# Output projection started on six of eight operand tiles, with the memory's keys and values computed beside its post-norm

## The chip, the cores and the metric

The kernel runs on one core of one Trainium2 chip. It is written by hand, engine by engine, with semaphores. Time is device microseconds of one execution: median 3300.87 us over three runs (3298.69 to 3303.33) for the kernel before. The profiled execution is a run of its own, of 3297.09 us.

## The reference, cut to what matters

A first block (512 tokens, width 1024, one layer) is followed by a second block of two layers. The change touches the middle of each of these two layers:

```python
def second_block(x, mem, ...):
    for l in range(2):
        h = rms_norm(x, mix_pre_g[l]);  proj = h @ w_in[l]
        ...                                            # latent attention (512 wide), gated unit (256 wide)
        o = rms_norm(diff_attention, g_sub) * (1 - lam_init)   # per head of 64; 256 wide
        mix = concat([out_a, out_b, o]) @ w_mix_out[l]         # 1024 x 1024
        x = x + rms_norm(mix, mix_post_g[l])
        h = rms_norm(x, mem_pre_g[l]);  mem_n = rms_norm(mem, mem_kv_g[l])   # mem: 256 tokens
        q = h @ mem_w_q[l];  k, v = split(mem_n @ mem_w_kv[l])
        x = x + rms_norm(attention(q, k, v) @ mem_w_o[l], mem_post_g[l])
        ...                                            # convolutional feed-forward
```

The keys and values need only `mem`, not `x`.

## The kernel before, in words

Activations lie features first: `[128, 8, 512]`, eight tiles `k` of 128 features by 512 tokens. The matrices come as a stream of slabs, 16 blocks of 128x128 each (1 MB). SyncE loads slab after slab into a ring of four (`feed`); ScalarE copies a slab's upper part to fp32r into a ring of two, `ring_hi` (`round`, L223), VectorE subtracts and leaves the lower part in place (`halve`, L230). A product is then three matmuls: upper by upper, upper by lower, lower by upper. Such three matmuls of one block are called a triple here. Activations are split the same way: ScalarE makes `hi`, VectorE (or GpSimd) `lo`. TensorE may begin a slab when `slab_split` has counted it; ScalarE may round the next one when `slab_begun` says that TensorE is past the slab whose place it takes. Each engine works off its instructions in order.

`stage(...)` puts one function on each engine between two barriers. In a layer the stages around the change are:

- `differential`: 16 units `u` of scores S (L1226), four transposes T (L1234), and for two units at once the values product V (L1243). VectorE takes maxima (L1282) and differences (L1292), ScalarE exponentials (L1265) and the copies of the turned tiles (L1271).
- `sub` (`norms`): the norm by heads of its result, `mix` tiles 6 and 7: two squares (L600), two sums on TensorE (L649), twice Ln and Exp, two products on VectorE (L670).
- `mix_out` (`project`, L1509): the eight `mix` tiles are split (L1528, L1541), output tile `n` = 8 triples into PSUM bank `n` (L281); beside it ScalarE squares finished banks (L730) and TensorE sums them (L736, two tiles behind). Then comes `PostNorm`: scale (L544, L546), new `x` on VectorE and GpSimd (L779, L784, L793), its squares (L766), eight sums (L744) and the next scale.
- `mem_qkv` (`linear`): `x` is normed and split, TensorE does four tiles of the query product (L412 to L414), sums the squares of `mem` (L649), does the other four, then eight key tiles of 256 columns and four value products of 512 columns in two groups (all L281).
- `memory`: the attention, which starts with GpSimd's copies (L1016).

The queries' slabs lie in the stream ahead of those of the keys and values, and all are loaded in that order.

## Time and profile before

| what | us |
|---|---|
| median of three runs | 3300.87 |
| profiled execution | 3297.09 |
| its span in the trace | 3295.3 |
| TensorE busy | 3002.6 |
| `differential` to the start of `memory`'s copies, first layer | 1541.41 to 1782.99 |

The span is what the trace shows of the execution; 1.8 us lie around it. Every time given below is counted from the start of the span. The two layers are the same instructions twice, so each figure of the first has its twin about 983 us later.

### The profile page before, as it was taken

How to read it: one execution, taken by the hardware profiler on the slowest of the kernel's cores; microseconds unless marked ns; L12 is line 12 of the kernel's file. 1: busy time of each engine (PE TensorE's matmuls, PEld its weight loads, DVE VectorE, ACT ScalarE, POOL GpSimd, SP SyncE). 2: the span in 40 equal slices, each digit the busy share in tenths (PEclk: the TensorE clock that was granted, in tenths of full speed). 3: DMA queues.
4: the chain of work that ended last, by engine and by line, in shares of the span. 5: the costliest groups of instructions: out<-in, count | busy, mean ns of one | idle time of the engine just before them, and what ended most of it. 6: DMA issues, size and time to landing. Idle time of an engine off the chain costs nothing. (4 is left out here: it accounts for less than half of the span.)

```text
span 3295.3 us, 39545 instructions
## 1 busy us (share of the span) xinstructions
PE 3002.6 (91%) x14872; PEld 2345.1 (71%) x14872; DVE 1519.0 (46%) x2143; ACT 1281.8 (39%) x1848; POOL 348.8 (11%) x299
## 2 busy tenths in 40 slices
PE   6989887999989989999789899988999889899998
PEld 2879765688768876675568678876775568578875
DVE  3356246565444433456444344433466444344432
ACT  3741434522243323435443333323435443433323
POOL 0110004500001100003011011100003011011100
PEclk8999999999999999999899999999999799999999
DMA  5100210044422222210122122221210122122222
GB/s 225 64 26 1 80 55 1 11 163 167 145 77 90 101 78 84 77 64 1 39 77 103 51 90 89 102 86 65 78 64 1 39 77 103 51 90 102 89 98 77
DMA packets 43554, 254.04 MB, mean 77 GB/s; under 512 B 4608, under 2 KB 6784, under 8 KB 15872
## 3 DMA queue, kind: packets, MB, share of 16 engines
q1 hardware_dynamic: 43392, 251.87, 21.5%
q8 instruction: 103, 1.69, 0.2%
q14 instruction: 59, 0.48, 0.1%
HBM read 249.75 MB, written 2.10 MB: 76 GB/s over the span
## 5 line engine op out<-in xcount | busy, mean ns | idle before, releaser
L230 DVE TENSOR_TENSOR ring_lo<-ring,ring_hi 128x2048 fp32r<-128x2048 f32 x201 | 460.6, 2292 | 934.7 <-ACT ring_hi L223 934.7
L281 PE MATMUL bank<-h_hi,ring_hi 128*128 128x512 f32 x1408 | 583.1, 414 | 55.6 <-DVE gated_lo L1488 26.1
L223 ACT ACTIVATE ring_hi<-ring 128x2048 fp32r<-128x2048 f32 x201 | 384.0, 1911 | 544.6 <-PE bank L281 400.7
L281 PE MATMUL bank<-h_hi,ring_lo 128*128 128x512 f32 x1408 | 556.4, 395 | 0.0
L1345 PE MATMUL bank<-h_hi,ring_hi 128*128 128x512 f32 x960 | 374.1, 390 | 5.8 <-DVE ring_lo L230 5.8
L1348 PE MATMUL bank<-h_lo,ring_hi 128*128 128x512 f32 x960 | 373.5, 389 | 0.0
L1349 PE MATMUL bank<-h_hi,ring_lo 128*128 128x512 f32 x960 | 373.5, 389 | 0.0
L281 PEld LDWEIGHTS bank<-h_hi,ring_hi 128*128 128x128 f32 x1408 | 268.6, 191 | 131.2 <-issue 55.7
L281 PEld LDWEIGHTS bank<-h_hi,ring_lo 128*128 128x128 f32 x1408 | 268.5, 191 | 63.4
L281 PE MATMUL bank<-h_lo,ring_hi 128*128 128x512 f32 x560 | 218.9, 391 | 0.0
L1345 PEld LDWEIGHTS bank<-h_hi,ring_hi 128*128 128x128 f32 x960 | 180.2, 188 | 45.8 <-issue 8.3
L281 PE MATMUL bank<-gated_lo,ring_hi 128*128 128x512 f32 x528 | 211.0, 400 | 0.0
L1349 PEld LDWEIGHTS bank<-h_hi,ring_lo 128*128 128x128 f32 x960 | 180.2, 188 | 37.3
L1348 PEld LDWEIGHTS bank<-h_lo,ring_hi 128*128 128x128 f32 x960 | 180.2, 188 | 37.3
L1416 DVE SCALAR_TENSOR_TENSOR mix<-bank,par,mix 128x511 f32<-128x511 f32 x176 | 123.8, 745 | 133.3 <-ACT mix L1393 126.3
L281 PE MATMUL bank<-mix_lo,ring_hi 128*128 128x512 f32 x336 | 143.1, 426 | 6.0 <-PEq L324 6.0
L281 PEld LDWEIGHTS bank<-h_lo,ring_hi 128*128 128x128 f32 x560 | 105.7, 189 | 25.1 <-issue 3.9
L1393 ACT ACTIVATE mix<-bank,par 128x512 f32<-128x512 f32 x88 | 63.7, 774 | 151.3 <-PE bank L1349 151.3
L281 PEld LDWEIGHTS bank<-gated_lo,ring_hi 128*128 128x128 f32 x528 | 100.9, 191 | 24.7 <-issue 2.4
L1430 POOL TENSOR_TENSOR gated<-mix 128x512 f32 (+1 forms) x44 | 57.0, 1296 | 427.5 <-ACT mix L1398 427.5
L1195 POOL TENSOR_TENSOR squares<-squares,stat 128x512 f32<-128x512 f32 x64 | 65.2, 1039 | 331.4 <-DVE stat L1157 331.4
L793 POOL TENSOR_TENSOR xT<-xT,raw 128x512 f32<-128x512 f32 x18 | 27.4, 1524 | 683.1 <-DVE raw L779 683.1
(415 smaller groups left out, 5105.4 us busy)
## 6 DMA issues: line engine op xcount, KB each, us to landing
ring<-in_stream SPq DMA_DIRECT2D x209, 1024.0 KB, 4.8
mod_w<-in_stream SPq DMA_DIRECT2D x64, 256.0 KB, 4.9
xT<-in_xT SPq DMA_DIRECT2D x2, 2048.0 KB, 14.9
const<-in_const SPq DMA_DIRECT2D x1, 2306.5 KB, 16.0
par<-in_par SPq DMA_DIRECT2D x3, 696.0 KB, 3.9
memT<-in_memT SPq DMA_DIRECT2D x2, 1024.0 KB, 4.7
out<-xT SPq DMA_DIRECT2D x1, 2048.0 KB, 6.3
ctxT<-in_ctxT SPq DMA_DIRECT2D x1, 1024.0 KB, 4.9
```

Of the source, the lines that this page charges most:

```text
L223: nc.scalar.activation(self.slab_hi(slab + j), self.slab(slab + j), ACT.Copy).then_inc(slab_rounded, 1)
L230: nc.vector.tensor_tensor(lower, self.slab(slab + j), self.slab_hi(slab + j).bitcast(F32), ALU.subtract)\
L281: ins = nc.tensor.matmul(out, lhsT, rhs, start=start and w is w_hi and x is x_hi, stop=stop and w is w_lo)
L793: nc.gpsimd.tensor_tensor(xT[:, n, :], xT[:, n, :], self.raw[:, n, :], ALU.add)\
L1195: nc.gpsimd.tensor_tensor(p, p, stat[:, u % 2, 2, g:g + 1].to_broadcast([P, p.shape[1]]), ALU.mult)\
L1345: first = nc.tensor.matmul(out_ap[s], w_hi, x_hi, start=k == 0, stop=False)
L1348: nc.tensor.matmul(out_ap[s], w_hi, x_lo, start=False, stop=False)
L1349: last = nc.tensor.matmul(out_ap[s], w_lo, x_hi, start=False, stop=k == KT - 1)
L1393: last = nc.scalar.activation(work[:, j % 2, s, :], out_ap[s], ACT.Identity, bias=conv_b(col), scale=conv_w(2 * FT + col))
L1416: last = nc.vector.scalar_tensor_tensor(w, out_ap[s][:, 1 - lo:T - lo], conv_w(col), w, ALU.mult, ALU.add)
L1430: nc.gpsimd.tensor_tensor(gated(n), work[:, j % 2, 0, :], work[:, j % 2, 1, :], ALU.mult)\
```

## The change

Three things are done in each layer. First, in `differential`, V of units `u-2` and `u-1` is issued ahead of T of unit `u`, not behind it. Second, the stage `sub` is gone, and `project` for `mix_out` is replaced by `mix_and_memory`: output tiles 0 and 1, then 2 and 3, first take their products with operand tiles 0 to 5, and the last two operand tiles follow when they are normed. Third, this same stage also norms and splits `mem`, and while the post-norm of `x` runs, TensorE does the keys and values; `mem_q` with only the queries is a stage of its own after it. GpSimd has no part in this post-norm, the slabs are loaded keys and values first, and some semaphores are shared.

```diff
+AT_MQ = B2_AT["mq"] + KV_SLABS * SLAB
+MQ_FIRST = B2_AT["mq"] // SLAB
+B2_AT["mk"], B2_AT["mv"] = B2_AT["mq"], B2_AT["mq"] + KT * KT
+assert B2_AT["mk"] % SLAB == 0
...
+                        place = g + APART
+                        if 0 <= s - MQ_FIRST < KV_SLABS:
+                            place += MQ_SLABS
+                        elif 0 <= s - MQ_FIRST - KV_SLABS < MQ_SLABS:
+                            place -= KV_SLABS
+                        src = stream[bass.ds(layer[0] * B2_SLABS + place, 1)].rearrange("o p n -> p (o n)")
...
+                if not by_pool:
+                    self.pool_tiles = ()
...
                 for u in range(N + 1):
                     if u + 2 < N:
                         scores(u + 2)
+                    if u >= 2 and u % 2 == 0:
+                        values(u - 2)
                     if u < N:
                         transposes(u)
-                    if u >= 2 and u % 2 == 0:
-                        values(u - 2)
...
+        def mix_and_memory(x, post, memT, mem_hi, mem_lo, k_out, v_out, h_gain, sub_gain, sync):
...
+            TILES, REST = 4, KT - 2
+            at, at_k, at_v = B2_AT["mix"], B2_AT["mk"], B2_AT["mv"]
+            first_k, first_v, first_q = at_k // SLAB, at_v // SLAB, (at_v + KT * KT) // SLAB
+            AHEAD = (4, 5, 6, 7, 0, 1, 2, 3)
...
+            k_banks = (1, 2, 3, 4, 5, 6, 7, 1)
+            v_banks = (2, 3, 4, 5)
...
+            def tensor(pe):
+                def key_tile(j):
+                    if j < len(LEFT):
+                        pe.wait_ge(y_left.sem, y_left.at(j + 1))
+                    elif j < KT - 1:
+                        pe.wait_ge(post.normed.sem, post.normed.at(j - len(LEFT) + 1))
+                    else:
+                        pe.wait_ge(k_read.sem, k_read.at(1))
+                    for k in range(KT):
+                        if j == 0:
+                            pe.wait_ge(mem_split.sem, mem_split.at(k + 1))
+                        last = ws.mm(pe, at_k + j * KT + k, 1, bank[:, k_banks[j], 0:MEM], (mem_hi[:, k, :], mem_lo[:, k, :]),
+                                     True, k == 0, k == KT - 1)
+                    last.then_inc(k_done.sem, 1)
...
+                def value_tiles(half):
+                    pe.wait_ge(k_read.sem, k_read.at(3 if half == 0 else 5))
+                    for k in range(KT):
+                        for tb in range(2):
+                            c = slice(tb * P, (tb + 1) * P)
+                            last = ws.mm(pe, at_v + half * 4 * KT + k * 4, 4, bank[:, v_banks[2 * half + tb], :],
+                                         (mem_hi[:, k, c], mem_lo[:, k, c]), False, k == 0, k == KT - 1)
+                    last.then_inc(v_done.sem, 1)
...
+                def first_tiles():
...
+                    for half in range(2):
+                        pe.wait_ge(slab_split, ws.count(first + half) - WHOLE_SLABS)
+                        for k in range(REST):
+                            for n in (2 * half, 2 * half + 1):
+                                begun = part_of(n, k)
+                                if k == 0 and n == 0:
+                                    begun.then_inc(slab_begun, 1)
+                            if half == 0 and k == 1:
+                                for g in range(2):
+                                    pe.wait_ge(sub_squared.sem, sub_squared.at(g + 1))
+                                    nc.tensor.matmul(bank[:, 6 + g, :], con("ones64"), post.squares[:, 2 + g, :], start=True, stop=True)\
...
+                    for n in range(TILES):
+                        for k in range(REST, KT):
+                            begun = part_of(n, k)
...
+                        if n >= 2:
+                            post.sum(pe, n - 2)
...
+                first_tiles()
+                for n in range(TILES, KT):
+                    if n == TILES:
+                        for k in range(KT):
+                            pe.wait_ge(mem_squared.sem, mem_squared.at(k + 1))
+                            last = nc.tensor.matmul(bank[:, 7, 0:MEM], con("ones"), mem_squares[:, k, :], start=k == 0, stop=k == KT - 1)
...
+                    for k in range(KT):
+                        last = ws.mm(pe, at + n * KT + k, 1, bank[:, n, :], x.part(pe, k), True, k == 0, k == KT - 1)
+                    last.then_inc(post.sum_done.sem, 1)
+                    if n >= 2:
+                        post.sum(pe, n - 2)
+                post.sum(pe, KT - 2)
+                post.sum(pe, KT - 1)
+                for j in range(5):
+                    key_tile(j)
+                next_sums(range(4))
+                for j in range(5, KT):
+                    key_tile(j)
+                next_sums(range(4, KT))
+                value_tiles(0)
+                value_tiles(1)
...
+                ws.round_to(act, at // SLAB, ws.limit)
+                upper(0)
+                upper(1)
+                for g in range(2):
+                    nc.scalar.activation(post.squares[:, 2 + g, :], x.whole[:, REST + g, :], ACT.Square).then_inc(sub_squared.sem, 1)
+                upper(2)
+                upper(3)
+                ws.round_second(act, at // SLAB + 1)
+                upper(4)
+                upper(5)
...
+                for g in range(2):
+                    act.wait_ge(sub_summed.sem, sub_summed.at(g + 1))
+                    nc.scalar.activation(sub_scale[g], bank[:, 6 + g, :], ACT.Ln, bias=con("eps", 1), scale=1.0 / 64)
+                act.drain()
+                for g in range(2):
+                    nc.scalar.activation(sub_scale[g], sub_scale[g], ACT.Exp, scale=-0.5).then_inc(sub_scaled.sem, 1)
+                upper(6)
+                upper(7)
+                act.wait_ge(sync.loaded.sem, sync.loaded.at(16))
...
+                for n in range(KT):
+                    ws.round_to(act, (at + n * KT + KT - 1) // SLAB + 1, ws.limit)
+                    post.square(act, n)
+                    if n in LEFT:
+                        leave(n)
...
+                ws.round_second(act, first_k + 1)
+                post.rms(act)
+                key_out(0)
+                key_out(1)
+                ws.round_to(act, first_k + 2, ws.limit)
+                next_squares((0, 1))
+                key_out(2)
+                key_out(3)
+                ws.round_to(act, first_k + 3, ws.limit)
+                next_squares((2, 3))
+                key_out(4)
+                next_squares((4, 5))
+                key_out(5)
+                ws.round_to(act, first_v, ws.limit)
+                next_squares((6, 7))
+                key_out(6)
+                key_out(7)
+                act.wait_ge(post.next_square_summed.sem, post.next_square_summed.at(KT))
+                root_of_mean(act, post.next_scale, bank[:, 0, :]).then_inc(post.next_scale_ready.sem, 1)
+                ws.round_to(act, first_v + 1, ws.limit)
+                round_h(range(4))
+                ws.round_to(act, first_v + 2, ws.limit)
+                round_h(range(4, KT))
+                value_out(0)
+                ws.round_to(act, first_v + 3, ws.limit)
+                ws.round_to(act, first_q, ws.limit)
+                value_out(1)
...
+            def vector(dve):
+                def new_x(n):
...
+                ws.halve_to(dve, at // SLAB, ws.limit)
+                for k in range(4):
+                    lower(k)
+                ws.halve_to(dve, at // SLAB + 1, ws.limit)
+                lower(4)
+                lower(5)
...
+                for g in range(2):
+                    dve.wait_ge(sub_scaled.sem, sub_scaled.at(g + 1))
+                    nc.vector.scalar_tensor_tensor(x.whole[:, REST + g, :], x.whole[:, REST + g, :], sub_gain, sub_scale[g],
+                                                   ALU.mult, ALU.mult).then_inc(sub_normed.sem, 1)
+                lower(6)
+                lower(7)
+                for n in range(KT):
+                    ws.halve_to(dve, (at + n * KT + KT - 1) // SLAB + 1, ws.limit)
+                    if n == 0:
+                        post.read_first(dve)
+                    if n == 4:
+                        dve.wait_ge(mem_scaled.sem, mem_scaled.at(1))
+                        for k in range(KT + 2):
...
+                ws.halve_to(dve, first_k + 1, ws.limit)
+                dve.wait_ge(post.scale_ready.sem, post.scale_ready.at(1))
+                dve.wait_ge(y_left.sem, y_left.at(len(LEFT)))
+                new_x(0)
+                new_x(1)
+                ws.halve_to(dve, first_k + 2, ws.limit)
+                new_x(2)
+                new_x(3)
+                new_x(4)
+                ws.halve_to(dve, first_k + 3, ws.limit)
+                new_x(5)
+                new_x(6)
+                new_x(7)
+                ws.halve_to(dve, first_v, ws.limit)
+                dve.wait_ge(post.next_scale_ready.sem, post.next_scale_ready.at(1))
+                norm_h(range(4))
+                ws.halve_to(dve, first_v + 1, ws.limit)
+                split_h(range(4))
+                norm_h(range(4, KT))
+                ws.halve_to(dve, first_v + 2, ws.limit)
+                split_h(range(4, KT))
+                ws.halve_to(dve, first_v + 3, ws.limit)
+                ws.halve_to(dve, first_q, ws.limit)
+            stage("mix_and_memory", tensor=tensor, scalar=scalar, vector=vector, sync=sync.issue)
...
-            norms("sub", [one_norm("o", lambda t, n=n: mix[:, 6 + n, :], lambda t: gain_sub, lambda t, n=n: mix[:, 6 + n, :], 1, T,
-                                   "ones64", 64) for n in range(2)], squares2, scales2)
...
-            project("mix_out", B2_AT["mix"], Split(h_hi, mix_lo, mix), post("mix_post"))
...
+            class Memory:
...
+                def issue(self, sp):
+                    sp.dma_start(self.dst, memT_in).then_inc(self.loaded.sem, 16)
...
+                mix_and_memory(Split(h_hi, mix_lo, mix), PostNorm(lambda n: p2("mix_post", 1, n), raw, squares2, scales2, by_pool=False),
...
+                h = Split(h_hi, h_lo)
+                linear("mem_q", [("act", T, weights_still(AT_MQ + n * KT, KT, h), act_copy(raw[:, n, :])) for n in range(KT)])
```

On TensorE, at the start of the output projection, this stands in the row before (`squares` by `const` are the sums of the norm by heads; `mix_lo` is an operand tile's lower part):

```order
L1243 MATMUL bank<-h_spare,dv 64x128 x7
L324 UNCONDITIONAL_BRANCH
L326 UNCONDITIONAL_BRANCH [waits barrier_Pool_Activation_PE_DVE_SP_release]
L648 ISA
L649 MATMUL bank<-squares,const 128x512 [waits square_ready_2]
L648 REGISTER_ALU
L649 MATMUL bank<-squares,const 128x512 [waits square_ready_2]
L324 UNCONDITIONAL_BRANCH
L326 UNCONDITIONAL_BRANCH [waits barrier_Pool_Activation_PE_DVE_SP_release]
L367 ISA
L203 ISA [waits operand_split_2]
L281 MATMUL bank<-h_hi,ring_hi 128x512 [waits slab_split]
```

And now, with L1639 to L1641 the three matmuls of a triple:

```order
L1258 MATMUL bank<-h_spare,dv 64x128 x7
L337 UNCONDITIONAL_BRANCH
L339 UNCONDITIONAL_BRANCH [waits barrier_Pool_Activation_PE_DVE_SP_release]
L1647 ISA
L380 ISA [waits slab_split]
L1639 MATMUL bank<-h_hi,ring_hi 128x512 [waits operand_split_2]
L1640 MATMUL bank<-mix_lo,ring_hi 128x512
L1641 MATMUL bank<-h_hi,ring_lo 128x512
...
L1656 MATMUL bank<-squares,const 128x512 [waits scored_2]
L1655 REGISTER_ALU
L1656 MATMUL bank<-squares,const 128x512 [waits scored_2]
L380 REGISTER_ALU
L1639 MATMUL bank<-h_hi,ring_hi 128x512 [waits operand_split_2]
```

One barrier is gone, and the two sums stand behind the first four triples, not ahead of them.

On VectorE, beside the value products, the order before holds only slabs' lower parts (L230) after the last copy of keys:

```order
L540 COPY mem_k<-bank 128x256 [waits tile_done_2]
L228 REGISTER_ALU
L230 TENSOR_TENSOR ring_lo<-ring,ring_hi 128x2048 [waits slab_rounded]
L228 REGISTER_ALU
L230 TENSOR_TENSOR ring_lo<-ring,ring_hi 128x2048 [waits slab_rounded]
L228 REGISTER_ALU
L230 TENSOR_TENSOR ring_lo<-ring,ring_hi 128x2048 [waits slab_rounded]
L324 UNCONDITIONAL_BRANCH
```

Now the norm and the split of `x` for the queries (L1796, L1802) stand among them (L238 is the slab's lower part):

```order
L238 TENSOR_TENSOR ring_lo<-ring,ring_hi 128x2048 [waits slab_rounded]
L1796 SCALAR_TENSOR_TENSOR hT<-xT,par,scales 128x512 [waits next_scale_ready_2]
L1796 SCALAR_TENSOR_TENSOR hT<-xT,par,scales 128x512 x3
L236 REGISTER_ALU
L238 TENSOR_TENSOR ring_lo<-ring,ring_hi 128x2048 [waits slab_rounded]
L1801 ISA
L1802 TENSOR_TENSOR h_lo<-hT,h_hi 128x512 [waits sum_read_2]
...
L1796 SCALAR_TENSOR_TENSOR hT<-xT,par,scales 128x512 x4
L236 REGISTER_ALU
L238 TENSOR_TENSOR ring_lo<-ring,ring_hi 128x2048 [waits slab_rounded]
L1801 REGISTER_ALU
L1802 TENSOR_TENSOR h_lo<-hT,h_hi 128x512 [waits sum_read_2]
```

The second slab of the values has moved behind four norm products, the third behind four lower parts and four more.

On TensorE in `differential`, the end of the stage before (T is L1234, V is L1243):

```order
L1232 REGISTER_ALU [waits probs_ready_2]
L1234 MATMUL bank<-const,squares 128x128 [waits probs_out0_2]
L1234 MATMUL bank<-const,squares 128x128 x3
L1240 REGISTER_ALU
L1243 MATMUL bank<-h_spare,dv 64x128 [waits probs_out0_2]
L1243 MATMUL bank<-h_spare,dv 64x128 x7
L1230 REGISTER_ALU
L1234 MATMUL bank<-const,squares 128x128 [waits probs_out0_2,probs_ready_2]
```

And now (T is L1249, V is L1258):

```order
L1255 REGISTER_ALU
L1258 MATMUL bank<-h_spare,dv 64x128 [waits probs_out0_2]
L1258 MATMUL bank<-h_spare,dv 64x128 x7
L1245 REGISTER_ALU
L1247 REGISTER_ALU [waits probs_ready_2]
L1249 MATMUL bank<-const,squares 128x128 [waits probs_out0_2]
L1249 MATMUL bank<-const,squares 128x128 x3
L1245 REGISTER_ALU
L1249 MATMUL bank<-const,squares 128x128 [waits probs_out0_2,probs_ready_2]
```

V has moved ahead of the wait for `probs_ready_2`.

## Rows read from the trace of the kernel before

**Rows 1.** The page: TensorE's busy time, and the granted clock in 40 slices.

```profile
PE 3002.6 (91%) x14872; PEld 2345.1 (71%) x14872; DVE 1519.0 (46%) x2143; ACT 1281.8 (39%) x1848; POOL 348.8 (11%) x299
...
PEclk8999999999999999999899999999999799999999
```

**Rows 2.** Windows: length, busy time of each engine, granted clock, DMA share, GB/s.

```profile
1432.88:1436.29 3.41, 3.18 (x8) 2.52 (x9) 0.41 (x1) 1.91 (x1) 0.00 (x0) 0.51 0.33 79
...
1538.00:1600.00 62.00, 47.95 (x292) 26.62 (x290) 44.04 (x85) 31.89 (x82) 0.00 (x0) 0.78 0.00 1
...
2523.60:2584.40 60.80, 48.55 (x256) 26.92 (x256) 42.66 (x83) 31.60 (x80) 0.00 (x0) 0.71 0.00 1
```

**Rows 3.** Timeline: start, length, instruction, idle before and releaser; `sub` to `memory`, both layers.

```profile
1599.83 1.15 ACT L600 ACTIVATE squares<-mix 128x512 f32<-128x512 f32 x2 [2.17 <-PEq L324]
...
1600.51 3.44 PE L649 MATMUL bank<-squares,const 128*128 128x512 f32 x4 [1.70 <-ACT squares L600]
...
1610.34 4.27 ACT L1528 ACTIVATE h_hi<-mix 128x512 fp32r<-128x512 f32 x8 [1.08 <-PEq L324]
1611.00 4.90 DVE L1541 TENSOR_TENSOR mix_lo<-mix,h_hi 128x512 fp32r<-128x512 f32 x8 [0.95 <-ACT h_hi L1528]
...
1611.83 0.79 PE L281 MATMUL bank<-h_hi,ring_hi 128*128 128x512 f32 x1 [7.88 <-DVE mix_lo L1541]
...
1782.99 1.04 POOL L1016 COPY h_spare<-raw 128x1024 f32 x1 [87.35 <-DVE stat L984]
...
2584.65 1.15 ACT L600 ACTIVATE squares<-mix 128x512 f32<-128x512 f32 x2 [3.05 <-PEq L324]
...
2766.28 1.04 POOL L1016 COPY h_spare<-raw 128x1024 f32 x1 [87.11 <-DVE stat L984]
```

**Rows 4.** Timeline of the post-norm and the norm before the queries, first layer.

```profile
1663.02 2.74 PE L736 MATMUL bank<-squares,const 128*128 128x512 f32 x6
1671.32 9.02 PE L744 MATMUL bank<-squares,const 128*128 128x512 f32 x16 [5.56 <-ACT squares L766]
1686.07 0.79 PE L412 MATMUL bank<-h_hi,ring_hi 128*128 128x512 f32 x1 [5.73 <-DVE h_lo L683]
...
1682.41 0.63 ACT L546 ACTIVATE scales<-scales 128x512 f32<-128x512 f32 x1
...
1683.33 2.08 DVE L670 SCALAR_TENSOR_TENSOR hT<-xT,par,scales 128x512 f32<-128x512 f32 x3 [3.85 <-PEq L324]
```

**Rows 5.** Timeline of the memory's projections: sums, first key, first and last value matmul, a slab's upper and lower part.

```profile
1710.82 3.61 PE L649 MATMUL bank<-squares,const 128*128 128x256 f32 x16
...
1736.05 0.28 PE L281 MATMUL bank<-mem_hi,ring_hi 128*128 128x256 f32 x1
...
1759.09 0.40 PE L281 MATMUL bank<-ring_hi,mem_hi 128*128 128x512 f32 x1
...
1765.12 1.92 ACT L223 ACTIVATE ring_hi<-ring 128x2048 fp32r<-128x2048 f32 x1 [3.68 <-PE bank L281]
...
1767.07 2.29 DVE L230 TENSOR_TENSOR ring_lo<-ring,ring_hi 128x2048 fp32r<-128x2048 f32 x1 [3.31 <-ACT ring_hi L223]
...
1781.25 0.40 PE L281 MATMUL bank<-ring_lo,mem_hi 128*128 128x512 f32 x1
```

**Rows 6.** Timeline: two matmuls in a row at the start of the output projection.

```profile
1616.25 0.63 PE L281 MATMUL bank<-mix_lo,ring_hi 128*128 128x512 f32 x1
...
1616.68 0.60 PE L281 MATMUL bank<-h_hi,ring_lo 128*128 128x512 f32 x1
```

**Rows 7.** Timeline of one pair of units in the differential attention.

```profile
1560.06 0.65 PE L1234 MATMUL bank<-const,squares 128*128 128x128 f32 x4 [1.29 <-DVE squares L1292]
1560.65 1.09 PE L1243 MATMUL bank<-h_spare,dv 128*64 128x128 f32 x16
1565.73 0.96 PE L1234 MATMUL bank<-const,squares 128*128 128x128 f32 x4 [1.29 <-DVE squares L1292]
...
1562.85 1.23 DVE L1282 TENSOR_REDUCE stat<-bank 128x2 f32<-128x1024 f32 x1 [0.25 <-PE bank L1226]
```

142 lines of the change are left out of this document (120 added, 22 removed).

## The prediction

> **What bounds the kernel now.** I read the page first: TensorE is busy for 91% of the span and the other engines for under half of it, and the granted clock is mostly full [rows 1]. So time comes off where TensorE stands still or runs at the lower clock. I then went through a layer in windows and found two such places beside the change: the differential attention, with a granted clock of 0.78 in the first layer and 0.71 in the second [rows 2], and the stretch from the output projection's last sum to the first query product, where TensorE does nothing but sums for 20 us and is busy for 9.0 of them [rows 4]. The timeline gives the ends of each piece. From the first square of the norm by heads to the start of the memory attention's copies it takes 1782.99 - 1599.83 = 183.2 us in the first layer and 181.6 in the second [rows 3]. The first layer's 183.2 fall into 12.0 before the first product (1611.83), 53.9 of output projection with eight sums (to 1665.76), 20.3 of post-norm and norm (to 1686.07), 50.0 of queries with the memory's sums inside (to 1736.05), 23.0 of keys (to 1759.09), 22.6 of values (to 1781.65) and 1.3 of closing [rows 3 to 5]. In the 12.0 and the 20.3 the chain goes through ScalarE and VectorE; TensorE has only sums in them.
>
> **The output projection begins earlier.** Before, the eight operand tiles were split after the norm, and the first product came 1.5 us after the first rounding (1610.34 to 1611.83) [rows 3]. Now tile 0 is split first, so TensorE starts about 1.5 us into the stage: 10.5 saved. It pays for this on its own queue: the two sums of the norm by heads stand behind the first four triples. At the lower clock they took 3.44 together [rows 3]; at full clock the three sums at the projection's end took 2.74, 0.91 each, so 1.8 [rows 4]. The stream will be turning from one clock to the other there, and I take 2.6, between the two. Are tiles 6 and 7 there in time? ScalarE does four roundings and two squares (0.53 each, eight took 4.27 [rows 3]), a slab (1.9), two roundings, then Ln and Exp: the scale is out at about 11.7, and the two norm products and lower parts end at 14.4. TensorE needs them after 48 triples, some 28 us in. Covered by 13 us; the cover is gone only if both halves lacked products. The `mem` squares (eight on ScalarE, behind tile 7) end near 16.5 and are needed at 30. The sums of `mem`, 3.6 [rows 5], move from the query stretch into this one, at the same price. Their DMA is issued at the start of the stage, ahead of SyncE's slabs, and is wanted 13 us later. Output projection with both kinds of sums: 53.9 + 2.6 + 3.6 = 60.1.
>
> **Keys beside the post-norm.** Ln and Exp with their table loads put a scale out 2.7 us after its last sum (1680.34 to 1683.04) [rows 4]. ScalarE now rounds a slab first, and not all of it fits beside the last two sums: I make it 3.7. TensorE has 8.6 us of keys to do before it wants the first bank back (key tile 3 waits for the first normed tile), so this is hidden by 4 us. Keys stay at 23.0 and the eight sums of the new squares come out of the gap onto the queue: 8 x 0.91 = 7.3. The tightest place is the third key slab: its upper part can begin when the second is begun (5.8 us into the keys), ScalarE is free at 6.3, 1.9 for the upper and 2.3 for the lower part [rows 5] make 10.5, and TensorE wants it at 11.5. I take no wait. GpSimd's three adds go to VectorE, which has the room between slabs.
>
> **Values beside the norm before the queries: a new wait.** The last sum and the start of the values are one moment, 0. The scale is out at 2.7. ScalarE then rounds the second value slab until 4.6; VectorE does four norm products (three took 2.08 [rows 4], so 2.7) until 5.5 and only then the slab's lower part, until 7.8. TensorE has gone through the first slab at 5.6 (half of a group's 11.3): it waits 2.2 us. The third slab's lower part stands behind four lower parts (eight took 4.90 [rows 3], so 2.4) and four more norm products: 7.8 + 2.4 + 2.7 + 2.3 = 15.2, wanted at 13.4: 1.8 us of waiting. The fourth comes at 15.2 + 2.4 + 2.3 = 19.9, wanted at 20.8. So the values cost 22.6 + 4.0 = 26.6. Behind VectorE's late slab TensorE's whole queue stands.
>
> **The rest.** A stage change now lies between values and queries: two copies and a barrier, about 2.0 us of idle TensorE. The queries' 64 triples take 64 x 3 x 0.232 = 44.5, the distance of two matmuls being 22.16 / 95 = 0.233 in the values [rows 5]. After such a pause the first eight matmuls of another stage ran at the lower clock, 0.51 of full for 3.4 us [rows 2]; at the lower clock two matmuls lie 0.43 apart (1616.25 to 1616.68) [rows 6], so eight lose 8 x 0.19 = 1.5 (0.43 less 0.233, rounded down). Last copy and barrier: 1.5. The new stretch is 1.5 + 60.1 + 23.0 + 7.3 + 26.6 + 2.0 + 44.5 + 1.5 + 1.5 = 168.0 us. Before: 183.2 and 181.6. Both layers save 28.8.
>
> **Values ahead of transposes.** In a pair of units TensorE waits 1.29 us for VectorE ahead of T of the even unit, then does T and V (1.09), and VectorE's next maximum waits 0.25 for scores that stand behind V [rows 7]. V now fills part of the idle 1.29 and the 0.25 goes, up to seven times; at the end of the stage one V less stands behind the last T, about 1.1. That is 1.4 at full clock, some 1 at the lower one, where TensorE itself is the bound, and more where the clock changes. I take 2.0 a layer. Bounds: nothing, and what full clock throughout would give: a pair takes 5.67 us there [rows 7], 16 units about 50 with start and end, against 58 and 61 now [rows 2], so 9 a layer.
>
> **The sum.** 28.8 + 4.0 = 32.8 us. The profiled execution took 3297.1, so 3264.3; it lies 3.8 below the median of the runs shown, and on that median the forecast is 3300.87 - 32.8 = 3268.
>
> **Rivals.**
> *The halving chain spreads (slower).* One mechanism: ScalarE's and VectorE's queues put a slab behind other work in all of its places, so that each of the six slabs from the third key slab to the last value slab is late. For: two of them are late by my own count, and the third key slab has only 1.0 us of room. Against: the chain itself (1.9 + 2.3) is shorter than the 5.6 us of a slab. The gain of 16.4 a layer is eaten at 16.4 / 6 = 2.7 us more per slab; at 4.0 more the layer loses 24 - 16.4 = 7.6, and the time is 3316. It decides from 2.7 us a slab on. 4%.
> *The waits bring the lower clock onto the values.* For: in the attention, where TensorE pauses 1.29 us in each pair, the granted clock is 0.71 to 0.78 [rows 2, 7]. Against: there it pauses all the time, here twice for about 2 us among full work. At the lower clock through all of the values their 96 matmuls would take 96 x 0.19 = 18.2 more, less the 4.0 of waiting, which VectorE then has time to avoid: 14 a layer, 3268 + 28 = 3296. 4%. With the lower clock for eight matmuls after each wait, 3.0 a layer, it is 3274; this is inside the likeliest case.
> *The clock stays up in the attention.* V fills the pause before which the clock used to fall. For: pauses get shorter. Against: TensorE still has less work than VectorE at full clock. Gain up to 7 more a layer: 3254. 12%.
> *The early start does not come off,* because something in front of the first product still waits for the norm by heads. The order shows one barrier and no such wait, so this is unlikely. It would give back 10.5 - 2.6 = 7.9 a layer: 3284. 5%.
>
> The Trainium skill, TensorE: Matmul & The Clock Gate, in "A second HAM failure mode: psum-queue depth-cycling", says that frequent short idle times between groups of matmuls make the clock swing and cost throughput even where matmuls look fast. The attention's 0.71 to 0.78 agrees with it; whether two waits among the values are frequent enough no row here shows. By this rule alone the second rival would hold, and the time would be its 3296.
>
> **How the numbers follow.** The likeliest case has 75%; its own range is 3257 to 3281, from the bounds of the attention (0 to 4 a layer), the two sums (1.8 to 3.4), the pause before the queries (0 to 3) and the value waits (2 to 8 with their clock). The range for 8 in 10 reaches into the cases on both sides: 3251 to 3285. A measurement of this kernel tells 0.2% (6.6 us) from no change. Faster by more than that is all up to 3294: 92%, the three cases of 3254, 3268 and 3284; within it, the case of 3296 and a light form of the spreading chain: 5%; slower: 3%.
>
> **What would show it.** Right: no sums of 512 columns before the first product, which comes within 2 us of the stage's start; TensorE without a gap from there to the values; 3 to 5 us of waits for slabs' lower parts in the values, and none in the keys; the stretch to the memory attention's copies 166 to 171 us; the differential stage 56 to 59 us. Wrong: waits for `ring_lo` in the keys, a clock below 0.9 over keys and values, or operand tiles 6 and 7 arriving after TensorE wants them.

## The result and the profile after

The changed kernel takes 3244.47 us (median of 4 runs, 3242.77 to 3246.44) against 3300.08 (3298.69 to 3303.33) for the kernel before on the same chip: a ratio of 0.9832, with a 95% interval of 0.9820 to 0.9844. It is 55.6 us faster; 32.8 were forecast, and the time lies below the range that was to hold it. The profiled execution of the changed kernel took 3246.4 us, with a span of 3244.6.

The page of the changed kernel first: TensorE's row, and the granted clock in 40 slices, beside [rows 1].

```profile
PE 2986.4 (92%) x14872; PEld 2332.4 (72%) x14872; DVE 1515.7 (47%) x2141; ACT 1282.1 (40%) x1866; POOL 327.4 (10%) x285
...
PEclk8999999999999999999799999999999899899999
```

The windows of the changed kernel, in order: differential attention, new stage and queries, for each layer. Columns as in [rows 2].

```profile
1539.83:1597.46 57.63, 48.98 (x256) 25.43 (x256) 42.66 (x83) 31.21 (x80) 0.00 (x0) 0.71 0.00 1
1597.46:1714.33 116.87, 110.54 (x532) 87.51 (x532) 61.46 (x71) 69.42 (x95) 0.00 (x0) 0.98 0.33 117
1714.33:1759.22 44.89, 43.81 (x192) 35.96 (x192) 9.17 (x4) 12.11 (x12) 0.00 (x0) 1.00 0.27 94
2495.66:2553.29 57.63, 48.98 (x256) 25.48 (x256) 42.65 (x83) 31.15 (x80) 0.00 (x0) 0.71 0.00 1
2553.29:2670.12 116.83, 110.47 (x532) 87.49 (x532) 61.47 (x71) 69.42 (x95) 0.00 (x0) 0.98 0.33 118
2670.12:2715.02 44.90, 43.82 (x192) 35.96 (x192) 9.17 (x4) 12.11 (x12) 0.00 (x0) 1.00 0.26 94
```

And the same stretches of the kernel before, cut from barrier to barrier in the same way:

```profile
1541.27:1599.75 58.48, 45.64 (x256) 24.72 (x256) 42.66 (x83) 31.61 (x80) 0.00 (x0) 0.77 0.00 1
1599.75:1782.49 182.74, 161.97 (x724) 127.81 (x724) 72.30 (x76) 81.03 (x98) 10.85 (x7) 0.93 0.28 98
2523.48:2584.57 61.09, 48.58 (x256) 26.97 (x256) 42.66 (x83) 31.60 (x80) 0.00 (x0) 0.71 0.00 1
2584.57:2765.80 181.23, 160.79 (x724) 126.86 (x724) 72.30 (x76) 81.03 (x98) 10.87 (x7) 0.93 0.28 99
```

The reader is to see three things. The stretch went from 182.74 to 116.87 + 44.89 = 161.76 us, and from 181.23 to 161.73 in the second layer: 40.5 us in all. Its 724 matmuls are the same 724; TensorE is idle for 7.4 us of it in place of 20.8, and the granted clock is 0.98 and 1.00 in place of 0.93. And the attention gave 0.85 us in the one layer and 3.46 in the other, with a clock no higher than before. The two spans differ by 50.6 us: 40.5 of the stretch, 4.3 of the attention, and 5.8 of stages that the change doesn't touch (see e7 and e8).

The timeline of the changed kernel, first layer: start of the stage with the two sums of the norm by heads, the first tile of the keys with the last sums ahead of it, the sums among the keys, the first value matmul, the two waits in the values, the first query product, the last one and the memory attention's first copy. It answers to [rows 3 to 5].

```profile
1597.54 1.15 ACT L1721 ACTIVATE h_hi<-mix 128x512 fp32r<-128x512 f32 x2 [2.81 <-PEq L337]
...
1598.94 0.80 PE L1639 MATMUL bank<-h_hi,ring_hi 128*128 128x512 f32 x1 [2.42 <-DVE mix_lo L1806]
...
1603.16 1.88 PE L1656 MATMUL bank<-squares,const 128*128 128x512 f32 x4
...
1654.23 2.74 PE L751 MATMUL bank<-squares,const 128*128 128x512 f32 x6
...
1656.40 0.68 PE L289 MATMUL bank<-mem_hi,ring_hi 128*128 128x256 f32 x1
...
1671.04 3.60 PE L1629 MATMUL bank<-squares,const 128*128 128x512 f32 x8
...
1686.04 0.79 PE L289 MATMUL bank<-ring_hi,mem_hi 128*128 128x512 f32 x1
...
1694.35 0.50 PE L289 MATMUL bank<-ring_hi,mem_hi 128*128 128x512 f32 x1 [2.14 <-DVE ring_lo L238]
1701.60 0.50 PE L289 MATMUL bank<-ring_hi,mem_hi 128*128 128x512 f32 x1 [1.39 <-DVE ring_lo L238]
1714.56 0.49 PE L289 MATMUL bank<-h_hi,ring_hi 128*128 128x512 f32 x1 [1.55 <-PEq L337]
...
1757.98 0.39 PE L289 MATMUL bank<-h_hi,ring_lo 128*128 128x512 f32 x1
...
1759.71 1.04 POOL L1031 COPY h_spare<-raw 128x1024 f32 x1 [223.45 <-DVE stat L999]
```

The mechanism is there step by step. The first product comes 1.40 us into the stage. Nothing waits between it and the values. The values wait twice for VectorE's half of a slab, 2.14 and 1.39 us, where 2.2 and 1.8 were forecast. What differs is the length of nearly every piece (us, first layer; a matmul's distance of 0.23 is added behind the last one):

| piece | forecast | measured |
|---|---|---|
| start to first product | 1.5 | 1.4 |
| output projection with its sums, sub sums, `mem` sums | 60.1 | 57.5 |
| keys and next sums | 30.3 | 29.6 |
| values with waits | 26.6 | 26.8 |
| stage change | 2.0 | 1.7 |
| 64 triples of queries | 44.5 | 43.6 |
| lower clock behind the stage change | 1.5 | 0 |
| close | 1.5 | 1.5 |
| sum | 168.0 | 162.2 (1759.71 - 1597.54) |

The clock explains most of it, 3.8 of the 5.8 us; the section on why the prediction was wrong in its size has the working. Two windows of the changed kernel, the first around the end of the attention and the first seven products, the second from there to the memory attention:

```profile
1594.90:1601.70 6.80, 4.38 (x23) 3.39 (x24) 3.28 (x5) 4.16 (x7) 0.00 (x0) 0.51 0.46 165
1601.70:1762.10 160.40, 151.97 (x721) 121.64 (x720) 68.12 (x72) 77.37 (x101) 1.80 (x3) 1.00 0.30 105
```

TensorE runs at 1.2 GHz until about 1601.9, and from there at 2.4 GHz without a break, over both waits and the stage change.

### The profile page after: what moved, and what is told of

Same layout as the page of the kernel before. It is cut to its first block and busy times, and to the rows that moved or that the text cites. A ratio compares the mean times of both kernels' runs of the same rounds, so it can differ in the third digit from the quotient of the medians.

```text
span 3244.6 us, 39481 instructions
## 1 busy us (share of the span) xinstructions
PE 2986.4 (92%) x14872; PEld 2332.4 (72%) x14872; DVE 1515.7 (47%) x2141; ACT 1282.1 (40%) x1866; POOL 327.4 (10%) x285
## 5 line engine op out<-in xcount | busy, mean ns | idle before, releaser
L238 DVE TENSOR_TENSOR ring_lo<-ring,ring_hi 128x2048 fp32r<-128x2048 f32 x201 | 460.6, 2291 | 909.1 <-ACT ring_hi L231 908.9
L1363 PE MATMUL bank<-h_lo,ring_hi 128*128 128x512 f32 x960 | 373.5, 389 | 0.0
L289 PE MATMUL bank<-h_lo,ring_hi 128*128 128x512 f32 x624 | 243.8, 391 | 0.0
L1363 PEld LDWEIGHTS bank<-h_lo,ring_hi 128*128 128x128 f32 x960 | 180.2, 188 | 37.4
L289 PEld LDWEIGHTS bank<-h_lo,ring_hi 128*128 128x128 f32 x624 | 117.8, 189 | 27.7 <-issue 3.9
L289 PE MATMUL bank<-mix_lo,ring_hi 128*128 128x512 f32 x272 | 116.6, 429 | 6.0 <-PEq L337 6.0
L1431 DVE SCALAR_TENSOR_TENSOR conv<-bank,par,conv 128x511 f32<-128x511 f32 x88 | 61.9, 745 | 66.6 <-ACT conv L1408 63.1
```

The source lines that it names most:

```text
L238: nc.vector.tensor_tensor(lower, self.slab(slab + j), self.slab_hi(slab + j).bitcast(F32), ALU.subtract)\
L289: ins = nc.tensor.matmul(out, lhsT, rhs, start=start and w is w_hi and x is x_hi, stop=stop and w is w_lo)
L1363: nc.tensor.matmul(out_ap[s], w_hi, x_lo, start=False, stop=False)
L1431: last = nc.vector.scalar_tensor_tensor(w, out_ap[s][:, 1 - lo:T - lo], conv_w(col), w, ALU.mult, ALU.add)
```

## Experiments

Medians of 4 or 5 runs each (e8 is one profiled run), and of 9 of the kernel before on the same chip; a ratio is that of the two, and its 95% interval is some 0.0014, or 4 to 5 us, to either side. "Stage" times are windows from barrier to barrier in one profile; "the stretch" is all from the attention's end to the memory attention. The changed kernel itself stands at 3244.5 (above) and 3246.1 (e7).

**e1: values back behind the transposes**

```diff
-                    if u >= 2 and u % 2 == 0:
-                        values(u - 2)
                     if u < N:
                         transposes(u)
+                    if u >= 2 and u % 2 == 0:
+                        values(u - 2)
```

> The changed kernel with the differential attention's values back behind the transposes; nothing else differs. The trace of the changed kernel has the attention 0.85 us shorter in the first layer (58.48 to 57.63) and 3.47 in the second (61.10 to 57.63). Theory A, the new order gives the 4.3 us that the trace shows: 3248.8 us, and the second layer's stage is again some 3 us longer than the first's. Theory B, the forecast's 2.0 a layer: 3248.5, with both stages about 59.6. Theory C, the order gives nothing and the stage's length only follows the granted clock: 3244.5, within 1. Theory D, the order is worth much more than the two traces show (7 a layer, so that it holds the part of the gain that lies outside the stretch): 3258.

3256.6 us (3254.6 to 3259.4), ratio 0.9871 (0.9856 to 0.9886): 12.1 more than the changed kernel (10.5 more than its repeat in e7). The attention took 62.00 and 57.84, together 4.6 more than in the changed kernel. The median is near D, the attention's sum near A (not its layers: the first is the longer one); no theory had both.

**e9: values ahead of the transposes, alone, in the kernel before**

> The kernel before with the values ahead of the transposes in the differential attention, and nothing else. Its stage took 58.5 to 62.0 us in six stages with the old order (mean 60.3) and 51.5 to 57.6 in fourteen with the new one (mean 56.2): 4.1 a layer. Theory A, the order alone does this: both stages at 57.6 or 51.5, the median 8 us below the kernel before, 3292, and up to 12 below if more executions than profiles have the short stage. Theory B, taking the values back cost 12.1 us in the changed kernel (3256.6 against 3244.5), and this belongs to both parts together: the order alone gives under 4, above 3296.

This is the kernel before with the two lines moved, nothing else. 3285.2 us (3283.6 to 3287.7) against 3299.6, ratio 0.9956 (0.9942 to 0.9970): 14.4 us. Both attention stages took 57.63. B has fallen: the order alone is worth what taking it back costs. A's size was too small again. The stretch of the changed kernel without it (e1) is then 43.1 us of the whole, and 12 to 14 are the order's.

**e7 and e8: the two kernels again**

> The changed kernel itself once more. The stages that the change doesn't touch take 2805.2 us together in its trace and 2811.0 in that of the kernel before; in the four variants so far 2808.4 to 2813.7. Theory A, these 5.8 us are chance of one execution: a second profile gives between 2805 and 2813, most likely above 2807. Theory B, they belong to the kernel (where the lower clock falls in later stages is set by how the stages before ended): again 2805.2 within 1. The median is 3244.5 within 1.5 by both.

> The kernel before itself, one more profile, for its untouched stages (2811.0 us in the first profile) and the differential attention (58.48 and 61.10). Theory A, chance of one execution: the untouched stages anywhere from 2807 to 2815. Theory B, it belongs to the kernel: 2811 within 1, and the attention's two stages as before.

The changed kernel gave 3246.1 (3244.3 to 3251.5), ratio 0.9833 (0.9819 to 0.9846). The windows of its new profile (attention, both layers), and then of the second profile of the kernel before:

```profile
1541.67:1599.30 57.63, 48.98 (x256) 0.71 0.00 1
2500.58:2558.12 57.54, 48.94 (x256) 0.71 0.00 1
```

```profile
1539.75:1601.74 61.99, 52.55 (x256) 0.67 0.00 1
2524.38:2584.84 60.46, 48.44 (x256) 0.72 0.00 1
```

The untouched stages (the span less the attention and the stretch of both layers) took 2810.8 and 2809.6 us in these, 2805.9 and 2811.7 in the first profiles; the expectations count each 0.7 lower. A, chance of one execution. e8's run took 3298.9. The stretch repeats within 0.2 us in the changed kernel (161.8, 161.9); the old one gave 182.5 twice in e8. Over four old and four new stretches the gain is 182.2 - 161.8 = 20.4 a layer. The old attention took 58.5, 61.1, 62.0, 60.5 here and 62.0, 57.8 in e1, mean 60.3; the new one 51.5 to 57.6 in 18 stages of nine profiles (all with the new order and no filling), mean 56.2.

**e10 and e11: TensorE filled where the attention makes it stand still**

e10 adds three matmuls on constants behind the first two score products. e11 adds three short ones ahead of each odd unit's transposes as well, and for this it exchanges the two waits there.

```diff
                 scores(1)
+                for _ in range(3):
+                    nc.tensor.matmul(bank[:, 5, :], con("ones"), const[:, 0:512], start=True, stop=True)
...
                 def transposes(u):
-                    pe.wait_ge(probs_ready.sem, probs_ready.at(u + 1))
                     if u >= 2:
                         pe.wait_ge(probs_out.sem, probs_out.at(u - 1))
+                    if u % 2:
+                        for _ in range(3):
+                            nc.tensor.matmul(bank[:, 5, 0:P], con("ones"), con("ident"), start=True, stop=True)
+                    pe.wait_ge(probs_ready.sem, probs_ready.at(u + 1))
```

> The changed kernel with three matmuls of 512 columns (constants by constants, into a bank that the first transposes overwrite) behind the first two score products of the differential attention, where TensorE stands still for 2.8 us. The stage's clock falls to half 3.9 to 4.2 us after its start in every profile so far, and stays there for 10.2 or for 27.3 us; the stage then takes 51.5 or 57.6. Theory A, that idle time is what brings the clock down: without it the long stretch at half clock goes, the stage takes 50 to 52 in both layers, 12 us in all, and the median is 3233 (less if part of the executions had the short stage already: 3236). Theory B, TensorE has too little work in the whole stage, and the clock falls a little later: 57 to 58, and the median 3244.5 to 3246.

> As the warm start, and three more matmuls of 128 columns (0.22 each at full clock) ahead of the transposes of each odd unit, where TensorE waits 0.76 to 0.88 us for VectorE once the clock is full. Theory A, the idle times inside the stage bring the clock down, and with these filled it stays full: 49 to 51 us a stage, 3230 to 3234. Theory B, the clock still falls, and then the added matmuls cost 8 x 1.3 = 10 us a stage at half clock, where TensorE is the bound: 60 to 67 a stage, above 3250.

e10 gave 3236.7 us (3234.1 to 3239.9), ratio 0.9811; e11 3232.1 (3228.3 to 3237.3), ratio 0.9799 (0.9785 to 0.9813). The start of the attention in the changed kernel, then in e11:

```profile
1539.92 1.14 PE L1241 MATMUL bank<-dk,dq 32*128 32x512 f32 x8 [1.06 <-PEq L337]
1543.85 2.08 PE L1241 MATMUL bank<-dk,dq 32*128 32x512 f32 x4 [2.78 <-ACT squares L1280]
```

```profile
1542.26 2.84 PE L1270 MATMUL bank<-const 128*128 128x512 f32 x6
1545.12 1.13 PE L1241 MATMUL bank<-dk,dq 32*128 32x512 f32 x4
```

The windows of the attention in e10, then in e11 (length, TensorE's busy time, granted clock):

```profile
1540.35:1589.19 48.84, 39.09 (x262) 0.97 0.00 1
2491.36:2544.72 53.36, 45.11 (x262) 0.84 0.00 1
```

```profile
1541.09:1589.12 48.03, 44.17 (x310) 1.00 0.00 1
2492.06:2540.08 48.02, 44.17 (x310) 1.00 0.00 1
```

A holds in both by the medians, and in e11 by the stages too. Four score matmuls take 2.08 us right behind the idle 2.78, and 1.13 when that time is filled. Work that nobody reads, 27 matmuls in e11 (each shows as two records: 310 against 256), takes 9.6 us off each layer's attention of 57.6: the clock stays at 2.4 GHz from end to end. The median gains less than twice that, 12.4 us (14.0 against e7); 1.2 GHz now comes right behind the stage, for 6.8 and 3.4 us, and the stretch takes 163.0 and 162.0, 1.5 more in both layers together. The second layer of e10 shows that the start alone is not enough: 0.84 and 53.36, outside A's 50 to 52.

**e13: the old order with the same filling**

> The kernel of the run with filler matmuls throughout the differential attention (3232.1 us, both stages 48.0), with the values back behind the transposes. Theory A, the order is worth its own queue places only, and the rest of the 12 to 14 us was clock: the forecast's terms at full clock, 0.25 up to seven times less on VectorE's chain and 1.1 at the end, are 1.4 to 2.8 a layer: 49.4 to 50.8 a stage, 3235 to 3238. Theory B, the order is worth 6 to 7 a layer at any clock: 54 to 55 a stage, 3244 to 3246. Theory C, with the old order the fillers no longer keep the clock up (the waits for VectorE were 1.29 us, longer than the 0.66 that the fillers take): 56 to 58 a stage, 3248 to 3252.

This is e11's kernel with e1's edit. 3237.3 us against 3303.0 (a chip on which the kernel before is 3.4 slower), ratio 0.9803 (0.9789 to 0.9816). Windows of its attention:

```profile
1541.65:1593.87 52.22, 44.32 (x310) 0.97 0.00 1
2490.64:2541.30 50.66, 42.76 (x310) 1.00 0.00 1
```

The profile lies a little above A: 4.2 and 2.6 us more than the 48.0 of e11, so 3.4 a layer (2.6 where the clock is 1.00). B and C are out. The medians of the two are too close to tell: 0.9803 and 0.9799, 1.3 us, with intervals of 4 to 5. So by the profiles 5 to 7 of the 12 to 14 us, about half at most, are what the order gives with the clock kept up; that the rest needs a clock that can fall is argued from this, not shown. The order's part is read from a pair of units at full clock, ahead of the odd unit's transposes, in the changed kernel:

```profile
1577.68 0.65 PE L1249 MATMUL bank<-const,squares 128*128 128x128 f32 x4 [0.85 <-DVE squares L1307]
...
1579.32 1.10 PE L1258 MATMUL bank<-h_spare,dv 128*64 128x128 f32 x16
...
1583.01 0.66 PE L1249 MATMUL bank<-const,squares 128*128 128x128 f32 x4 [0.88 <-DVE squares L1307]
```

A pair takes 1583.01 - 1577.68 = 5.33 us, and 5.67 before [rows 7]. The pause of 1.29 is down to 0.87.

**e6: a longer pause ahead of the queries**

```diff
+                def copy_again(n):
+                    nc.scalar.activation(post.squares[:, n, :], bank[:, v_banks[2 + n % 2], :], ACT.Copy)
...
                 value_out(1)
+                for n in range(4):
+                    copy_again(n)
```

> The changed kernel with four more copies of 512 columns on ScalarE (0.54 each, into square tiles that nothing reads) at the end of the stage ahead of the queries, so that TensorE stands still for about 3.9 us there and not 1.7. My forecast took eight matmuls at the lower clock after the pause, 1.5 us; the trace of the changed kernel shows none after 1.7 us, while the memory attention, after 3.35 us, begins at the lower clock. Theory A, the length of the pause decides, and the longer one brings the lower clock: 2.2 + 1.5 a layer, 3252. Theory B, the pause costs its own length and the full clock goes on: 2.2 a layer, 3249.

3254.2 us (3252.5 to 3257.7), ratio 0.9859. The last value matmul, the first query product, two of the later ones, and a window that begins with these two:

```profile
1713.26 0.40 PE L289 MATMUL bank<-ring_lo,mem_hi 128*128 128x512 f32 x1
1717.17 0.49 PE L289 MATMUL bank<-h_hi,ring_hi 128*128 128x512 f32 x1 [3.51 <-PEq L337]
...
1718.69 0.63 PE L289 MATMUL bank<-h_hi,ring_hi 128*128 128x512 f32 x1
1719.11 0.63 PE L289 MATMUL bank<-h_lo,ring_hi 128*128 128x512 f32 x1
```

```profile
1718.60:1722.00 3.40, 3.40 (x9) 0.50 0.87 306
```

Counted like the 1.7 before, to 0.23 behind the last value matmul's start, the pause is 1717.17 - 1713.49 = 3.7 us (the expectation has 3.9), and the clock goes to half for eight matmuls. The stretch takes 165.5 in both layers, 3.7 more: 2.1 of pause (the stage ends 118.9 us into the stretch in place of 116.9) and 1.6 of clock (the queries' stage takes 46.5 in place of 44.9). That is A, and 1.6 is near the forecast's 1.5 us; the price was right and its place was not.

**e2, e3, e4: each part of the stretch undone**

e2 puts the norm by heads ahead of the first slab and the first product, e3 all next sums ahead of the keys (`next_sums(range(KT))`, then the eight key tiles, with the other engines' orders to match), e4 lets the values wait for the last rounded tile (ScalarE and VectorE then norm, round and split all eight tiles ahead of the slabs; not shown):

```diff
                     pe.wait_ge(k_read.sem, k_read.at(3 if half == 0 else 5))
+                    if half == 0:
+                        pe.wait_ge(h_rounded.sem, h_rounded.at(KT))
```

> The changed kernel with the norm by heads put ahead of everything else in the new stage: two squares, two sums, the scale, and only then the first slab, the first rounding and the first product. Working: squares 1.1, sums 1.7, Ln and Exp 2.7, slab 1.9, rounding and lower part 1.1 put the first product at 8.5 us after the stage's start, not 1.4: 7.1 later, less 1.7 for the sums that leave TensorE's queue, so 5.4 a layer and 3255. Theory A, a longer pause also lengthens the stretch at the lower clock (before, it reached 5.3 us into the products, now 2.8), about 1.4 more a layer: 6.8 a layer, 3258. Theory B, the pause costs its own length only: 3255. Theory C, the start was not the source of the gain because VectorE's and ScalarE's queues behind it (tiles 6 and 7, the sums of mem) were late anyway: 3248 or less.

> The changed kernel with the whole post-norm (eight new tiles, squares and their sums) ahead of the first key tile. Working: in the changed kernel the scale is out at 1660.9, 4.5 us after the keys begin; eight new tiles take 8 x 1.37 = 11.0, the last square and sum 1.5, so the keys begin 16.9 us later; 6.9 of sums leave the queue beside them: 10.0 a layer. Theory A, a pause of this length brings the lower clock at its end, 1.5 to 3 more a layer: 11.5 to 13 a layer, 3267.5 to 3270.5. Theory B, no clock effect: 3264.5. Theory C, the keys only hid work that TensorE waits for later (the values would wait longer for their slabs): under 7 a layer, below 3258.5.

> The changed kernel with the norm before the queries whole ahead of the values: TensorE waits until the eighth normed tile is rounded, then does the values. Working: the scale is out 3.3 us after the values would begin, eight norm products take 5.5, the last rounding 0.6: 9.4 a layer; the two waits inside the values (2.1 and 1.4) shrink to about 0.9: 6.8 a layer, 3258. Theory A, the pause brings the lower clock onto the first values, 1.5 more: 8.3 a layer, 3261. Theory B, the waits inside the values stay: 9.4 a layer, 3263. Theory C, the gain of this part is small, since the waits in the values are its other side: 4 a layer or less, 3252. If the four parts are independent and hold all of the change, the four losses (this one, the late start, the late keys, the values behind the transposes) add up to 55.6 us.

| run | us | ratio (95%) | loss | stretch, both layers |
|---|---|---|---|---|
| e2 | 3257.0 | 0.9868 (0.9853 to 0.9883) | 12.5 | 169.0, 168.5 |
| e3 | 3271.9 | 0.9911 (0.9897 to 0.9924) | 27.4 | 173.9, 175.1 |
| e4 | 3264.2 | 0.9891 (0.9876 to 0.9906) | 19.8 | 169.4, 169.8 |

Behind each longer pause the first work runs at the lower clock: in e2 the first product and its 0.79 us, in e3 the first sums (eight records in 5.48 us, in the changed kernel 3.60), in e4 the first value matmul.

```profile
1610.26 0.79 PE L1639 MATMUL bank<-h_hi,ring_hi 128*128 128x512 f32 x1 [4.52 <-DVE mix_lo L1805]
```

```profile
1665.66 5.48 PE L1629 MATMUL bank<-squares,const 128*128 128x512 f32 x8 [6.23 <-ACT squares L1707]
```

```profile
1701.58 0.79 PE L289 MATMUL bank<-ring_hi,mem_hi 128*128 128x512 f32 x1 [8.91 <-ACT h_hi L1718]
```

In the stretch each loss is near A's, with 6.9, 12.7 and 7.8 a layer for 6.8, 11.5 to 13 and 8.3. The medians of e3 and e4 are 2 and 4 us above twice that, the one of e2 1 below. The four losses add up to 71.8, not 55.6: an undone part isn't the old code, and each longer pause brings its own stretch of lower clock.

**e5 and e12: the two pauses that are left**

e5 rounds and halves the value slabs ahead of the norm's work; e12 puts the 64 query triples into the same stage, in banks 0, 1, 6, 7, 2, 3, 4, 5. Of e5's edit:

```diff
+                ws.round_to(act, first_v + 1, ws.limit)
                 act.wait_ge(post.next_square_summed.sem, post.next_square_summed.at(KT))
...
+                ws.halve_to(dve, first_v + 1, ws.limit)
                 dve.wait_ge(post.next_scale_ready.sem, post.next_scale_ready.at(1))
                 norm_h(range(4))
-                ws.halve_to(dve, first_v + 1, ws.limit)
+                ws.halve_to(dve, first_v + 2, ws.limit)
                 split_h(range(4))
+                ws.halve_to(dve, first_v + 3, ws.limit)
                 norm_h(range(4, KT))
...
```

> The changed kernel with the value slabs' roundings and halvings ahead of the norm before the queries: ScalarE rounds the second value slab before it takes the scale, and VectorE halves the second slab before the first four norm products, the third before the first four lower parts, the fourth before the last four norm products. Theory A, the two waits inside the values (2.14 and 1.39 in the first layer) are all that the norm's place costs, and they go: 3.5 a layer, 3237.5 us. Theory B, the wait only moves: the norm's last lower parts end 6 us later and the first query product waits for them or for its slab; the gain is 0 to 1 a layer, 3243 to 3244.5. Theory C, the pauses in the values also cost clock that the trace hides: 5 a layer or more, below 3234.5.

> The changed kernel with the queries' projection inside the new stage: the first query product follows the last value product without the two copies and the barrier, in other banks. TensorE's pause there is 1.7 us in the changed kernel (1712.9 to 1714.6). Theory A, the pause goes: 1.7 a layer, 3.4 us, 3241. Theory B, the slab behind the pause was what it waited for, and the time stays: 3244.5. Theory C, VectorE's lower parts or a bank are late, up to 2 a layer slower: 3248.

e5: 3238.7 us (3235.7 to 3249.4), ratio 0.9822 (0.9808 to 0.9835), 5.8 to 7.3 below the changed kernel; no wait for a slab is left in the values, and the stretch takes 158.0 in the first layer. A. In the second (159.3) the lower clock reached 5.7 us into the first products, because the attention ahead had ended otherwise. e12: 3241.5 us (3241.4 to 3246.9), ratio 0.9830 (0.9816 to 0.9843), 2.9 to 4.5 below. The median is A's, but both ratios' intervals overlap that of the changed kernel (0.9820 to 0.9844), and for e12 the profile gives A in one layer only: the stretch takes 160.0, 1.8 less, and 161.4, 0.3 less, where 1.2 GHz reached 6 us into the first products and not 3.

**e14: joined**

> Three versions joined: filler matmuls throughout the differential attention (12.4 us below the changed kernel's 3244.5), the value slabs ahead of the norm before the queries (5.8 to 7.3) and the queries in the same stage (2.9 to 4.5). Theory A, they touch different places and add up: 21 to 24, so 3221 to 3223. Theory B, the queries right behind the values now wait for the lower parts that the norm leaves last, and the last two share one gain: 3225 to 3228.

3223.2 us (3219.5 to 3224.6) against 3303.0, ratio 0.9757 (0.9743 to 0.9770), the fastest kernel here. A: the gains add up (12.4, 5.8 and 2.9 make 21.1; it is 21.3 below the changed kernel). TensorE waits 0.8 us for one slab in the joined stage, which takes 158.5 and 158.6 us with the queries, and the attention 48.1 in both layers.

## Why the prediction was wrong in its size

The direction, the mechanism and the new waits were right and no slower rival came. Two terms of the gain were sized too small, and 3244.5 lies below the range of 3251 to 3285.

**"The new stretch is 1.5 + 60.1 + 23.0 + 7.3 + 26.6 + 2.0 + 44.5 + 1.5 + 1.5 = 168.0 us."** It measured 162.2, and the old one 182.2, so a layer gained 20.4 and not 14.4: 12 of the 22.8 us missed. Of the 5.8 a layer, 3.8 are the lower clock put where it was not: 1.5 for "after such a pause the first eight matmuls of another stage ran at the lower clock", 0.9 for the two sums taken between both clocks (2.6, measured 1.7 with the step back to the product: at full clock all along), and 1.4 since the old 53.9 of projection held more of the lower clock (5.3 us of its products, now 2.9: about 1.2 of the 1.4) than the new 52.5. The other 2 us are roundings to the safe side: the queries at the values' distance of 0.232 (their own is 0.227: 0.9), the sums at their whole length of 0.91 and not at their distance of 0.86 (0.7 with the keys), the `mem` sums and the stage change (0.3 each), less 0.2 in the values.

The forecast took the price of 1.5 from the first window of [rows 2] and didn't ask how long TensorE had stood still before it, which was 2.98 us; the new pause is 1.55 by the same count, and e6 got its eight matmuls with 3.51. Of the kernel before:

```profile
1433.11 0.79 PE L281 MATMUL bank<-mix_lo,ring_hi 128*128 128x512 f32 x1 [2.98 <-PEq L324]
```

**"I take 2.0 a layer. Bounds: nothing, and ... 9 a layer."** The order is worth 12.1 us taken back and 14.4 alone, so 6 to 7 a layer: 8 to 10 of the 22.8. The measured value is inside the bounds and far from the 2.0. The step counted only VectorE's wait of 0.25 a pair. A pair became 0.34 shorter at full clock, the stage 2.6 to 3.4 (e13). Part of the rest came with the clock: the old order takes 57.8 to 62.0 with 34 us of a stage at 1.2 GHz on average, the new one 51.5 to 57.6 with 29, and the same new one with the clock kept up 48.0. The case "the clock stays up" (12%, 3254) was true in a small part: in most stages the clock is 0.71 as before. Its price "up to 7 more a layer" was the right bound for it; what came is 4 to 5 more than the 2.0, and not shown to be clock alone.

With both terms at their measured size the sum is 3297.1 - 40.9 - 12 to 14 = 3242 to 3244 for the profiled execution's own time, and 3246 to 3248 on the median of 3300.9; 3244.5 was measured. That this meets the measured time is no proof of the second term: the attention's profiles account for 8.2 of its 12 to 14 us, and the other 4 to 6, no more than a ratio's interval, remain open.

Step by step otherwise: the first product within 2 us (1.4), operand tiles 6 and 7 in time, no wait in the keys, 3 to 5 us of waits in the values (3.5), the attention 56 to 59 (57.6): right. The last was luck in part: this profile shows about the forecast's gain of 2.0 a layer (4.3 in both), while other profiles have stages of 51.5, and the runs gave three times as much. Stretch 166 to 171: wrong, 162. One working was wrong without harm: TensorE wants tile 6 after 24 triples, not 48, at 1618.75. VectorE's last two lower parts end at 1611.0, so the cover was 7.7 us and not 13:

```profile
1609.65 1.35 DVE L1806 TENSOR_TENSOR mix_lo<-mix,h_hi 128x512 fp32r<-128x512 f32 x2
...
1618.75 0.40 PE L1639 MATMUL bank<-h_hi,ring_hi 128*128 128x512 f32 x1
```

**The second rival** put the lower clock onto the values after two waits of 2 us. The trace has clock 1.00 there, but its light form, "the lower clock for eight matmuls", is real: of the 18 layers profiled with the changed kernel's order of the value slabs (its two profiles, e1, e2, e6, e10 to e13), 8 have the clock at half for 3.4 us, from within 1.4 us of the end of the first wait. The second layer of e7:

```profile
2654.95:2658.35 3.40, 3.22 (x8) 2.55 (x9) 3.40 (x7) 2.09 (x2) 0.00 (x0) 0.50 0.36 75
```

It costs next to nothing, and not the 3.0 a layer of the forecast: in all 8 the second wait of 1.4 us is gone (the other 10 have it), since VectorE's slab is ready when the slower TensorE comes to it, and the stretch takes 161.9 in place of 161.8 (in e6, 165.5 with and without). The Trainium skill, TensorE: Matmul & The Clock Gate, "A second HAM failure mode: psum-queue depth-cycling", says that frequent short idle times between groups of matmuls make the clock swing. In the values the traces show the clock falling behind a single wait in some layers, at no cost. In the attention they show the swing and its cost: idle times of 0.3 to 2.8 us between groups, clock 0.71, and 48.0 us in place of 57.6 once they are filled (e11).

## What to carry to other kernels

When a stage with short pauses runs at 0.7 of the clock, price each pause twice, by its length and by the matmuls behind it at double distance, and look at how long the pause before that level was: the same price applied to a pause of half the length was wrong here. A lower clock ahead of a wait for another engine costs only what is left when that wait is used up. Fill what pauses remain with matmuls that nobody reads, first behind the stage's first products: moving two lines gave 12 to 14 us in the medians, and a few filler matmuls another 12 to 14. And repeat a profile before explaining 5 us in stages that the change doesn't touch.

## What the runs showed of the hardware

- Filler matmuls on constants hold the granted clock at 1.00 through a stage that had 0.67 to 0.83 in every profile without them (e11). VectorE and ScalarE beside it are busy for 41.9 and 31.1 us, 42.7 and 31.2 without.
- The same code mostly takes one of two lengths: the attention 57.6 us (13 of 18 stages) or 51.5 (3), with the clock at half for 27.3 or 10.2 us behind its first wait; the other two took 56.2 and 52.6. In e5 both stand in one execution; the windows are the two stages, and the half-clock part of each:

```profile
1539.12:1596.75 57.63, 48.98 (x256) 0.71 0.00 1
2494.67:2546.22 51.55, 42.08 (x256) 0.83 0.00 1
```

```profile
1543.10:1570.40 27.30, 27.25 (x106) 0.50 0.00 1
2498.80:2509.10 10.30, 10.30 (x39) 0.50 0.00 0
```

- A pause of 1.7 us between two stages full of matmuls left the clock at 2.4 GHz in all 20 layers profiled; the wait of 2.14 us in the values brought 1.2 GHz in 8 of 18; a pause of 3.7 us brought 1.2 GHz for 3.4 us in both layers, beginning 1.5 us after the work had begun again (e6).
